# A two-model transformer kernel on one Trainium2 core: norms behind residuals done in two halves of the tokens

## What is computed

```
for l in range(2):                                    # first network
    u = h * (1 + sc1) + sh1;  y = mixer(u)            # attention, mLSTM, w_out
    h = layer_norm(ALPHA * h + g1 * y, ln1_g, ln1_b)  # r0 -> n1, r2 -> n3
    u = h * (1 + sc2) + sh2;  y = swiglu(u)
    h = layer_norm(ALPHA * h + g2 * y, ln2_g, ln2_b)  # r1 -> n2, r3 -> n4
# second network: x + gate * f(rms_norm(x) * (1 + sc) + sh)
# norms n5 (in front of the LRU/stick-breaking mixer), n6 (ffn), n7 (window attention), n8 (ffn)
layer_norm: mu = mean(x); var = mean((x - mu)**2); (x - mu) / sqrt(var + eps) * g + b
rms_norm:   x / sqrt(mean(x * x) + eps) * g
```

## Time and profile before

| | |
|---|---|
| time, median of 3 runs | 3771.4 us (3764.7 to 3777.4) |
| the profiled execution | 3772.4 us, its span 3770.4 us |
| PE, DVE, ACT, POOL busy | 94%, 42%, 36%, 39% of the span |
| mean granted clock of PE | 0.971 |
| read from HBM | 379 MB, 101 GB/s |

### The profile page before, as it was taken

How to read it: one execution, slowest core, us unless ns; L and a number is a source line. 1 busy time by engine, 2 the same in 40 slices (tenths; PEclk the granted TensorE clock), 3 DMA queues, 4 the chain that set the end, 5 groups by cost and what they waited for, 6 DMA issues and landing times.

```text
span 3770.4 us, 39245 instructions
## 1 busy us (share of the span) xinstructions
PE 3562.2 (94%) x16132; PEld 2784.7 (74%) x16132; DVE 1593.4 (42%) x2122; ACT 1346.2 (36%) x2185; POOL 1473.7 (39%) x788
## 2 busy tenths in 40 slices
PE   7999999998999899999899899988889999999999
PEld 5887767876888688766687788855567887777887
DVE  4436564354442333665435544255544312444220
ACT  4444444223231344444322323245532222543321
POOL 2333333444554333333344445423124444224543
PEclk9999999999999999999999999999889999999999
DMA  6333212544554234321154455422015332212332
GB/s 206 106 101 118 60 41 56 143 131 131 166 164 137 67 101 123 101 56 45 53 143 128 141 161 159 120 75 73 6 56 158 104 95 80 76 57 84 95 95 73
DMA packets 566977, 385.28 MB, mean 102 GB/s; under 512 B 13598, under 2 KB 504302, under 8 KB 566798
## 3 DMA queue, kind: packets, MB, share of 16 engines
q1 hardware_dynamic: 564574, 379.56, 34.4%
q10 hardware_dynamic: 2224, 3.21, 0.3%
HBM read 379.25 MB, written 2.10 MB: 101 GB/s over the span
## 4 chain that ended last, share of the span: by engine, by line
PE 80%; DVE 9%; ACT 6%; POOL 2%; issue 1%; DMA 1%; SPq 0%; ACTq 0%; DVEq 0%; POOLq 0%
PE ps L174 79%; POOL wlo L144 2%; ACT whi L140 1%; DVE nrm L149 1%; ACT L136 1%; PE ps L178 1%; DVE nrd L155 1%; DVE nrm L144 1%; DVE H L152 1%; DVE ST L158 1%; DVE mq L152 0%; ACT sxb L136 0%; DVE UL L144 0%; DVE ACC L152 0%; DVE sp L152 0%
## 5 line engine op out<-in xcount | busy, mean ns | idle before, releaser
L144 POOL TENSOR_TENSOR wlo<-raw,whi 128x1024 fp32r<-128x1024 f32 (+1 forms) x540 | 1281.5, 2382 | 1945.8 <-ACT whi L140 1945.4
L174 PE MATMUL ps<-UH,whi 128*128 128x512 f32 x2656 | 1072.1, 404 | 55.9 <-ACT UH L140 37.6
L174 PE MATMUL ps<-UH,wlo 128*128 128x512 f32 x2656 | 1050.4, 395 | 22.2 <-POOL wlo L144 22.2
L174 PE MATMUL ps<-UL,whi 128*128 128x512 f32 x2656 | 1049.3, 395 | 5.0 <-DVE UL L144 3.8
L140 ACT ACTIVATE whi<-raw 128x1024 fp32r<-128x1024 f32 (+1 forms) x540 | 546.4, 1023 | 521.3 <-PE ps L174 229.1
L174 PEld LDWEIGHTS ps<-UH,whi 128*128 128x128 f32 x2656 | 506.8, 191 | 183.1 <-ACT UH L140 44.5
L174 PEld LDWEIGHTS ps<-UH,wlo 128*128 128x128 f32 x2656 | 506.9, 191 | 143.7 <-POOL wlo L144 34.0
L174 PEld LDWEIGHTS ps<-UL,whi 128*128 128x128 f32 x2656 | 506.0, 190 | 123.0 <-DVE UL L144 12.3
L152 DVE SCALAR_TENSOR_TENSOR ACC<-raw,SM,ACC 128x512 f32<-128x512 f32 x308 | 359.9, 1169 | 20.5 <-DVE fg L144 0.5
L174 PE MATMUL ps<-GH,whi 128*128 128x512 f32 x704 | 274.9, 390 | 0.0
L174 PE MATMUL ps<-GL,whi 128*128 128x512 f32 x704 | 274.1, 389 | 0.0
(11 more groups left out here) (331 smaller groups left out, 4202.3 us busy)
## 6 DMA issues: line engine op xcount, KB each, us to landing
raw<-in_w_in SPq DMA_DIRECT2D x168, 512.0 KB, 4.2
...
```

The costliest lines, as they stand in the source:

```text
L144: return self.e.tensor_tensor(o, a, b, op).then_inc(*self.done(*keys))
L174: m = self.e.matmul(o, l, r, start=start, stop=stop)
```

## The change

Tokens 0 to 255 are half 0, 256 to 511 half 1 (`HALF`). `HALVED` says how many of a residual's last tiles are made half by half: two (r0, r2, r4, r6) or one (r1, r3, r5).

- **PE.** The fills of the halved tiles come first, then the half 0 of each tile, the first fp32 products of half 0's sums (`pe_norm_first`), four input tiles of half 1 of the first halved tile, the last fp32 products (`pe_norm_last`), and the rest of half 1. The pair behind the norm is made in halves (`pe_beside_norm`), and half 1's sums stand in it behind input tile `late(rid) + 1`.
- **Means.** In LayerNorm, after tile 1 of the residual, a product with ones over H0 + H1 (`pm`) gives a rough mean, which DVE takes off each tile as it comes (Hc). So squares are made during the residual (N2) as well as sums (N1). In the norm the rest of the mean, d, is taken off again (`dve_again`), and its square off the variance.
- **Norm.** Root, reciprocal, scaling, modulation, UH and UL are done half by half. The modulation has moved from DVE to ACT (`act_u`, two instructions a tile and half). UF, over UL's place, is its fp32 result.
- **n4 and n5** are interleaved: half 0 of n5 beside half 1 of n4, with ACT adding the bias.
- **n2.** The pair is now the first two q/k tiles; the V rows come behind, with the edge blocks last, for which ACT and DVE copy the edges once (`act_ends`, `dve_ends`).

The diff, cut to its core:

```diff
+    HALF = (slice(0, 256), slice(256, 512))
+    def pe_half(p, job, x, ks, KT, XH, XL, xw=None):
+        key, o, cs = job
+        c = HALF[x]
+        if o is None:
+            o = ps(key + (x,))
+        for k in ks:
+            j, n = divmod(k, 8)
+            i, ends_chunk = cs[j], n == min(8, KT - 8 * j) - 1
+            q = split_slot(i)
+            wh, wl = (t[q][:, n * 128:(n + 1) * 128] for t in (his, los))
+            p.wait_ge(*on("act", "hi", i))
+            if xw:
+                p.wait_ge(*xw(k)[0])
+            p.mm(o[:, c], wh, XH[:, k, c], k == 0, False)
+            p.wait_ge(*on("pool", "lo", i))
+            p.mm(o[:, c], wl, XH[:, k, c], False, False)
+            if xw:
+                p.wait_ge(*xw(k)[1])
+            keys = [("used", i)] if x and ends_chunk else []
+            if k == KT - 1:
+                keys += [key + (x,)] + ([key] if x else [])
+            p.mm(o[:, c], wh, XL[:, k, c], False, k == KT - 1, *keys)
...
+    HALVED = {"r0": 2, "r1": 1, "r2": 2, "r3": 1, "r4": 2, "r5": 1, "r6": 2, "r7": 0}
+    N1, N2, N3 = (at(f"np{i}", 88 + 2 * i, [128, S]) for i in range(3))
+    NX = at("npx", 94, [128, 256])
+    def late(rid):
+        return 1 if HALVED[rid] == 2 else 3
+    def pe_norm_first(p, nid, x, means):
+        c = HALF[x]
+        if x == 0 and means:
+            bank(p, AUX, ("s1", nid), ("dve", ("d", nid, 1)))
+        if x == 0:
+            bank(p, AUX, ("s2", nid), ("dve", ("var", nid, 1)) if means else ("act", ("sd", nid, 1)))
+        if means:
+            p.wait_ge(*on("dve", "p1", nid, x))
+            p.mm(ps(("s1", nid))[:, c], ones, N1[:, c], True, False)
+        p.wait_ge(*on("dve", "p2", nid, x))
+        p.mm(ps(("s2", nid))[:, c], ones, N2[:, c], True, False)
+    def pe_norm_last(p, nid, x, means):
+        c = HALF[x]
+        if means:
+            p.wait_ge(*on("dve", "Hc", nid, NT - 1, x))
+            p.mm(ps(("s1", nid))[:, c], ones, H[:, NT - 1, c], False, True, ("s1", nid, x))
+        p.wait_ge(*on("act", "sq", nid, NT - 1, x))
+        p.mm(ps(("s2", nid))[:, c], ones, N3[:, c], False, True, ("s2", nid, x))
+    def pe_beside_norm(p, rid, nid, means, jobs, group):
+        js = [pe_open(p, *job, group) for job in jobs]
+        for x in range(2):
+            for k in range(NT):
+                for job in js:
+                    pe_half(p, job, x, (k,), NT, UH, UL, xu(nid, x))
+                if x == 0 and k == late(rid) + 1:
+                    pe_norm_first(p, nid, 1, means)
+                    pe_norm_last(p, nid, 1, means)
+    def dve_last(v, rid, nid, gate, means, m, x):
+        c = HALF[x]
+        v.wait_ge(*on("pe", rid, m, x))
+        v.stt(H[:, m, c], ps((rid, m, x))[:, c], gate[:, m:m + 1], H[:, m, c], ALU.mult, ALU.add,
+              ("H", rid, m, x), ("H", rid, m) if x else None)
+        if means:
+            v.wait_ge(*v.prior())
+            v.stt(H[:, m, c], ps(("pm", nid))[:, c], -1.0 / 256, H[:, m, c], ALU.mult, ALU.add,
+                  ("Hc", nid, m, x), ("Hc", nid, m) if x else None)
+            if m < NT - 1:
+                v.wait_ge(*v.prior())
+                v.tt(N1[:, c], N1[:, c], H[:, m, c], ALU.add, ("p1", nid, x))
...
+    def dve_rest(v, nid, x):
+        c = HALF[x]
+        v.wait_ge(*on("pe", "s1", nid, x))
+        v.ts(N1[:, c], ps(("s1", nid))[:, c], -1.0 / D, None, ALU.mult, None, ("d", nid, x))
+    def dve_again(v, nid, kt, x):
+        c = HALF[x]
+        v.wait_ge(*on("dve", "d", nid, x))
+        v.tt(H[:, kt, c], H[:, kt, c], N1[:, c], ALU.add, ("Hr", nid, kt, x))
+    def dve_variance(v, nid, x):
+        c = HALF[x]
+        v.wait_ge(*on("act", "ds", nid, x))
+        v.stt(N3[:, c], ps(("s2", nid))[:, c], 1.0 / D, N3[:, c], ALU.mult, ALU.subtract, ("var", nid, x))
+    def dve_root(v, nid, R, x):
+        c = HALF[x]
+        v.wait_ge(*on("act", "sd", nid, x))
+        v.recip(R[:, c], R[:, c], ("root", nid, x))
+    def dve_scaled(v, nid, kt, x, g):
+        c = HALF[x]
+        v.wait_ge(*on("dve", "root", nid, x))
+        if g is None:
+            v.tt(UF[:, kt, c], H[:, kt, c], N1[:, c], ALU.mult, ("h", nid, kt, x))
+        else:
+            v.wait_ge(*on("dve", "Hr", nid, kt, x))
+            v.stt(H[:, kt, c], H[:, kt, c], g[:, kt:kt + 1], N3[:, c], ALU.mult, ALU.mult, ("h", nid, kt, x))
+    def half_lo(e, nid, kt, x):
+        if lo_lane(nid, kt) == e.name:
+            e.wait_ge(*on("act", "uh", nid, kt, x))
+            e.tt(UL[:, kt, HALF[x]], UF[:, kt, HALF[x]], UH[:, kt, HALF[x]].bitcast(F32), ALU.subtract, ("ul", nid, kt, x))
+    def dve_first_half(v, rid, nid, gate, means, g, lo):
+        R, b0 = (N3 if means else N1), late(rid)
+        if means:
+            dve_rest(v, nid, 0)
+            dve_again(v, nid, 0, 0)
+            dve_again(v, nid, 1, 0)
+            dve_variance(v, nid, 0)
+            dve_again(v, nid, 2, 0)
+        if HALVED[rid] == 2:
+            dve_last(v, rid, nid, gate, means, 6, 1)
+        dve_root(v, nid, R, 0)
         for kt in range(NT):
+            if means and kt + 3 < NT:
+                dve_again(v, nid, kt + 3, 0)
+            dve_scaled(v, nid, kt, 0, g)
+            if kt:
+                lo(kt - 1)
+            if kt == 0 and HALVED[rid] == 2:
+                dve_add(v, nid, 6, 1)
+            if kt == b0:
+                dve_last(v, rid, nid, gate, means, 7, 1)
+            if means and kt == b0 + 3:
+                dve_rest(v, nid, 1)
+            if means and kt == b0 + 4:
+                dve_again(v, nid, 0, 1)
+                dve_variance(v, nid, 1)
+                dve_again(v, nid, 1, 1)
+        lo(NT - 1)
+        if means:
+            dve_again(v, nid, 2, 1)
+        dve_root(v, nid, R, 1)
...
+    def act_u(a, nid, kt, x, means):
+        c = HALF[x]
+        u = UF[:, kt, c]
+        a.wait_ge(*on("dve", "mod", nid))
+        a.wait_ge(*on("dve", "h", nid, kt, x))
+        blk, _, jsh = mod_of(nid)
+        a.af(u, H[:, kt, c] if means else u, ACT.Identity, ("u", nid, kt, x), scale=S1[:, kt:kt + 1],
+             bias=B1[:, kt:kt + 1] if means else ad(blk, jsh, kt, 1))
+        a.wait_ge(*a.prior())
+        a.cp(UH[:, kt, c], u, ("uh", nid, kt, x))
+    def act_first_half(a, rid, nid, means, second, tile):
+        if means:
+            act_variance(a, nid, 0)
+        act_root(a, nid, 0, means)
+        if HALVED[rid] == 1:
+            act_split(a, lin_end[second] + 1)
+        else:
+            act_sq(a, rid, nid, means, 6, 1)
+        for kt in range(NT):
+            tile(kt)
+            if kt == late(rid):
+                act_sq(a, rid, nid, means, 7, 1)
+            if means and kt == late(rid) + 3:
+                act_variance(a, nid, 1)
+            if kt == late(rid) + 4:
+                act_root(a, nid, 1, means)
+    def act_norm(a, rid, nid, means, first, second):
+        act_first_half(a, rid, nid, means, second, lambda kt: act_u(a, nid, kt, 0, means))
+        for kt in range(NT):
+            act_u(a, nid, kt, 1, means)
+            if kt == 1:
+                act_split(a, soon(*first))
...
+        jobs = []
+        for m in range(NT - n, NT):
+            if fill:
+                pe_fill(p)
+            jobs.append(pe_open(p, (rid, m), name, lay, m * 128, None, LIN4, KT))
+        for m, job in zip(range(NT - n, NT), jobs):
+            bank(p, LIN4, (rid, m, 0), ("dve", ("H", rid, m, 0)))
+            pe_half(p, job, 0, range(KT), KT, XH, XL)
+        pe_norm_first(p, nid, 0, means)
+        for j, job in enumerate(jobs):
+            m = NT - n + j
+            bank(p, LIN4, (rid, m, 1), ("dve", ("H", rid, m, 1)))
+            pe_half(p, job, 1, range(KT) if j else range(4), KT, XH, XL)
+            if j == 0:
+                pe_norm_last(p, nid, 0, means)
+                pe_half(p, job, 1, range(4, KT), KT, XH, XL)
...
+        added = {3: (1,), 4: (2, 3), 5: (4,), 6: (5,)}
+        for m in range(NT - n):
             if fill:
                 dve_fill(v)
             v.wait_ge(*kept(m))
             v.wait_ge(*on("pe", (rid, m)))
             v.stt(H[:, m, :], ps((rid, m))[:, :], gate[:, m:m + 1], H[:, m, :], ALU.mult, ALU.add, ("H", rid, m))
+            if means:
                 v.wait_ge(*v.prior())
+                if m == 1:
+                    v.tt(N1[:, :], H[:, 0, :], H[:, 1, :], ALU.add, ("part", nid))
+                if m > 1:
+                    v.wait_ge(*on("pe", "pm", nid))
+                    for t in range(3) if m == 2 else (m,):
+                        v.stt(H[:, t, :], ps(("pm", nid))[:, :], -1.0 / 256, H[:, t, :], ALU.mult, ALU.add, ("Hc", nid, t))
+                if m > 2:
+                    v.wait_ge(*v.prior())
+                    ks = [("p1", nid, 0), ("p1", nid, 1)] if m == NT - 2 else []
+                    v.tt(N1[:, :], H[:, 2, :] if m == 3 else N1[:, :], H[:, m, :], ALU.add, *ks)
+                for t in added.get(m, ()):
+                    dve_add(v, nid, t)
+            elif sums == "squares" and m > 1:
```

(37 more changed lines are left out.)

470 lines of the change are left out of this document (254 added, 216 removed).

## The result

Over four runs each the changed kernel takes 3806.15 us at the median (3797.75 to 3809.47), the kernel before 3771.54 (3764.72 to 3777.37). The ratio is 1.0089, with a 95% interval of 1.0064 to 1.0114: by the medians 35 us slower, where +9 was forecast. A second set of runs of the same kernel gave 1.0089 again (1.0066 to 1.0111). The profiled execution has a span of 3801.5 us, 31.1 longer than before.

A forecast was written before the change was run, and what follows sets the result against it. PE bounds the kernel nearly everywhere, but DVE's norm end (LayerNorm), or ACT and DVE in turns (RMS), ends a boundary. Terms 4.9 - 1.6 + 4.9 - 6.5 + 1.0 - 0.6 + 3.9 + 3.4 = +9: 3780, range 3742 to 3815.

The forecast's parts named there:

- the clock rival: Thin half products keep PE at 1.2 GHz behind the pairs: 4.7 us at each of seven boundaries, total 3811; chance 0.17.
- What stands ahead of 0: Three costly moves, (1), (2) and (3), ahead of 0, which is the end of tile 7's first half.
- (2): In r0, tile 7's weights are needed earlier and come later; 0 at 839.6 instead of 834.5, 5.1 us.
- (3): In r2, both fills precede tile 6, so PE waits for DVE's ACC; 0 at 2059.5 instead of 2053.4, 6.1 us.
- (1): POOL's wlo delay DVE's adds of squares and PE's sums: 2.7 us at n6 and n8, 1.8 n3, 3.5 n1.
- The walk through a boundary: LayerNorm: DVE ends 35.0 us after 0, before 36.7; PE's idle head 2.5, not 17. RMS: near 26.5 plus split chunks.
- with nothing in their way: At n2, V rows (96 products, 21.7 us) follow PE's pair unhindered; 60.5 against 62.1, -1.6 us.
- the one clear gain: At n4 with n5, two norms overlap: 50.7 against 57.2, -6.5 us.
- The prices: At half width: DVE 0.35 to 0.42 us, ACT 0.50 with pointers, POOL 0.73, reciprocal 1.7; two half products 0.0125 more.
- One body after POOL's end: Beside POOL, a blocked DVE instruction ends one body after POOL's end, whatever its size.
- Faster: Rival: POOL's half instructions fit into DVE's waits for ACT; two thirds of 41 us gone, 3752; chance 0.28.
- Nothing changes: Rival: DVE bounds both kernels, stalls of (2) and (3) are absorbed; sum -2, 3769; no separate chance, within the forecast's spread.

## Why the prediction held within its range and was short in size

It forecast 3780 with 3742 to 3815, and slower, same and faster nearly alike. 3806 lies inside that range, but beyond the forecast's own 3766 to 3794; it is inside only because the range was stretched to the clock rival at 3811, whose mechanism had 6 of its 31 us. That is luck and not insight, and so is the sign: +9 was less than the 11 us that the prediction itself couldn't tell from nothing. The table has what each boundary moved the start of the next residual by, counted from its own residual's start, in the first and the second profile (sums before rounding; the forecasts with one product pm of 0.86 at each LayerNorm):

```
            n1    n2    n3    n5    n6    n7    n8    sum
forecast   +5.8  -0.7  +5.8  -5.6  +1.0  -0.6  +3.9   +9.4
measured   +9.3  +4.0 +10.7  -4.4  +5.1  +1.8  +3.2  +29.8
again      +9.0  +7.9 +10.8  -2.0  +2.8  -0.8  +4.5  +32.1
```

- **"What stands ahead of 0", (2) and (3): right mechanisms, mis-sized.** Tile 7's first half was to end 47.7 us behind r0's start and 48.0 behind r2's; it ended at 51.9 (50.4 again) and 54.4. I gave the late weights 5.1 and the columns 6.1; by the same clock they cost 9.3 and 12.5. Left out in both: DVE's fill is itself held up by POOL (2.79 in r0 and 2.77 in r2 for 0.75), and one more chunk is late (PE waits 1.60 for tile 6's in r0, 1.43 for tile 5's in r2, and for neither in the kernel before). PE also fell to 1.2 GHz in or after these waits (23 and 26 half products, 0.09 us more each, 2.1 and 2.4); the prediction had 1 for that at n3 and nothing at n1.
- **(1), the adds behind POOL: right in the mechanism, the price right at n6 alone.** PE waits 3.08 at n6 and 1.55 at n8 for a forecast 2.7 at each. At n1 it waits 1.09 for a forecast 3.5 and at n3 0.14 for 1.8: there PE comes so late by (2) and (3) that the adds are nearly done. The stalls were added up where they overlap. The sequel at n6 was missed: 1.2 GHz, and DVE's update of tile 6 ahead of the reciprocal. From 0 to DVE's end n6 took 35.5 (33.5 again) for a forecast 31.0; n8 took 32.0 for 32.7.
- **The walk through a boundary: right within 3 us.** From 0 to DVE's end n1 took 37.1 for a forecast 38.5, n3 35.4 for 34.4, n7 30.5 for 30.0. Without the waits of (1) the walk itself had 35.0 and 32.6 at n1 and n3, and took 36.0 and 35.2, so part of the agreement is two errors that cancel. At the long residuals DVE's end does not move: at n2, n5 and n7 it is within 0.9 us of before. PE's idle head did go (2.0 us at n1 for 17) and came back inside the pair.
- **n2: wrong sign.** The V rows were to follow "with nothing in their way". They start 1.81 us late, behind a split and a copy on ACT, and the next chunk behind them is 1.39 late: 3.2 of the 4.7 by which the forecast missed in the first profile. DVE's end itself is where it was. No run takes this wait away.

```profile
1283.88 0.50 PE L174 MATMUL ps<-whi,UH 128*128 128x512 f32 x1 [1.81 <-ACT qk L140]
...
1307.32 0.47 PE L174 MATMUL ps<-UH,whi 128*128 128x512 f32 x1 [1.39 <-ACT VA L140]
```

- **n5, "the one clear gain": wrong.** DVE's end came 0.3 and 0.9 us earlier, not 6.5. From 0 it took 54.4 for 50.7, 0 itself is 1.5 later by pm and the half products, and some 0.8 lies in the 57.2 for the kernel before, which runs past DVE's end there. Of the 3.7, ACT's scaling with pointers has a part (0.60 us for my 0.50); the rest is not settled.
- **The prices: right but that one.** The reciprocal at 256 took 1.748 us for an estimated 1.7, a POOL half 0.73 to 0.76 alone, a DVE half beside POOL 0.95. "One body after POOL's end" is a little too much: the DVE instruction of the rows below ends 0.28 behind POOL's, with a body of 0.48, and in r4 the add of 0.69 ends 0.54 behind.
- **The sum has slips of its own.** The 4.9 of the half products, worked out under the prices, is not among its eight terms; n6 has 2.5 where (1) says 2.7; and 4.7 at each of seven boundaries is 33, not 31. None of them changes what was forecast by more than 5 us.
- **Half products.** r5 is the clean case: PE without a gap, 121.3 us for 119.5. Its 66 halved products at 2 x 0.12 for 0.2265 give 0.9, two fp32 products of 0.43 the other 0.9. The rule of the Trainium skill that I weighed ("TensorE: Matmul & The Clock Gate", Back-to-back issue gap) gives an estimate of 0.2 for the 66; the trace decides for the row.

**The rivals.** *Faster* falls: beside POOL a DVE half takes 0.95 for 0.48, and the run with all low parts on DVE was not slower. The trace agrees with the rule on the port in the Trainium skill ("SBUF — State Buffer", Who interferes with whom): size was no help.

```profile
857.96 0.94 POOL L144 TENSOR_TENSOR UL<-UF,UH 128x256 fp32r<-128x256 f32 x1 [10.96 <-ACT UH L140]
858.23 0.95 DVE L152 SCALAR_TENSOR_TENSOR H<-H,VT,np 128x256 f32<-128x256 f32 x1
```

*Slower by the clock* has the time (3811) mostly for the wrong reason. Its test was the clock behind a pair, 0.5 for over 5 us. Windows of 18 us behind n1, n3 and n6, first the changed kernel, then the kernel before:

```profile
882.30:900.00 17.70, 15.88 (x71) 13.16 (x71) 5.51 (x9) 5.32 (x7) 4.71 (x2) 0.87 0.72 207
...
2116.00:2134.00 18.00, 10.92 (x38) 8.36 (x37) 10.61 (x10) 7.21 (x9) 7.94 (x3) 0.72 0.84 245
2842.00:2860.00 18.00, 13.16 (x51) 10.85 (x50) 8.89 (x14) 3.66 (x6) 2.37 (x1) 0.81 0.48 147
```

```profile
873.00:891.00 18.00, 15.59 (x65) 12.58 (x65) 7.16 (x10) 4.89 (x8) 6.04 (x3) 0.91 0.71 204
2092.00:2110.00 18.00, 12.00 (x39) 9.29 (x40) 8.82 (x8) 5.85 (x7) 9.33 (x4) 0.72 0.87 262
2815.00:2833.00 18.00, 12.43 (x43) 10.31 (x44) 8.22 (x11) 2.31 (x3) 3.40 (x2) 0.72 0.48 146
```

0.87 for 0.91, 0.72 for 0.72, 0.81 for 0.72: no fall against the kernel before. Taken by its words the test can't decide: 0.72 over 18 us is some 10 us at 0.5, so it is met behind n3 and n6 in the kernel before as well. What the clock did cost lies in the halved tiles, which the rival named in brackets: some 6 us in r0, r2 and r4 together. *Nothing changes* (3769 without the stalls of (2) and (3)) falls too: the stalls were not absorbed, and the kernel in which both are mostly gone still takes 3782, 11 us above the kernel before.
